# Placing the expert loop of a two-block transformer at an instruction-block boundary on TensorE

## The reference, cut to what matters

```python
logits = (t @ w_router) + b_router                 # 256 tokens, 8 experts
top_v, top_e = lax.top_k(logits, 2)
gate = softmax(top_v)
# for each expert e, over the tokens that chose it:
y += gate * ((silu(x @ w_gate[e]) * (x @ w_up[e])) @ w_down[e])   # 1024 -> 3584 -> 1024
```

## Time and profile before

| what | value |
|---|---|
| median of 3 runs | 3565.04 us (3564.34 to 3575.8) |
| the profiled execution: its time, its span | 3575.8 us, 3574.0 us |
| TensorE matmuls, busy share of the span | 96% |
| mean granted TensorE clock, as a share of 2.4 GHz | 0.964 |
| DMA of weights and data | 637.61 MB |
| packets of the instruction queue q8, bytes | 81, 1.33 MB |

### The profile page before, as it was taken

The page is one execution under the profiler, slowest core; times in us unless marked ns, Lnnn a source line. Parts: engine busy times, 40 slices in busy tenths (PEclk is TensorE's granted clock), DMA queues, the critical chain, the costliest instruction groups (busy, mean ns, idle before and its releaser), DMA issues.

```text
span 3574.0 us, 76004 instructions
## 1 busy us (share of the span) xinstructions
PE 3419.3 (96%) x32714; PEld 2833.5 (79%) x32715; DVE 775.5 (22%) x1802; ACT 679.7 (19%) x1469; POOL 93.0 (3%) x141
## 2 busy tenths in 40 slices
PE   8999799999999999999999999979999999999998
PEld 4456658884557788887788887779999999988898
DVE  1214636650103321213210113230100110011000
ACT  2224122220113321212210111211111111110011
POOL 0000000010001010100000010000000000000000
PEclk9999689999899999999999999979999999999999
DMA  6446012212223243332344442229999998944476
GB/s 271 177 153 236 3 48 83 89 73 73 77 94 113 97 151 132 127 134 103 122 144 141 139 145 106 103 97 370 373 352 371 354 371 346 361 172 153 145 272 264
DMA packets 94763, 637.61 MB, mean 178 GB/s; under 512 B 10784, under 2 KB 11824, under 8 KB 38592
## 3 DMA queue, kind: packets, MB, share of 16 engines
q1 hardware_dynamic: 92048, 627.58, 47.6%
q0 software_dynamic: 2608, 8.49, 0.7%
HBM read 634.98 MB, written 1.05 MB: 178 GB/s over the span
## 4 chain that ended last, share of the span: by engine, by line
PE 93%; DVE 3%; DMA 2%; ACT 2%; issue 1%; SPq 0%; ACTq 0%; DVEq 0%
PE bank L528 24%; PE bank L950 20%; PE bank L620 18%; PE bank L571 7%; PE bank L640 5%; PE bank L542 4%; PE bank L907 2%; PE bank L476 2%; PE bank L502 1%; PE bank L676 1%; PE bank L965 1%; PE bank L658 1%; PE bank L665 1%; DMA ring<-in_moe_down 1%; PE bank L1016 1%
## 5 line engine op out<-in xcount | busy, mean ns | idle before, releaser
L528 PE MATMUL bank<-H,ring 128*128 128x256 f32 (+1 forms) x3040 | 775.0, 417 | 6.9 <-ACT H L1124 6.2
L528 PEld LDWEIGHTS bank<-H,ring 128*128 128x128 f32 x3040 | 580.5, 192 | 185.3 <-issue 112.3
L620 PE MATMUL bank<-PROJ,ring 128*64 128x96 f32 (+2 forms) x7776 | 667.1, 282 | 12.4 <-ACT SC L1173 9.6
L620 PEld LDWEIGHTS bank<-PROJ,ring 128*64 128x64 f32 (+1 forms) x7776 | 547.1, 147 | 131.0 <-issue 96.8
L950 PE MATMUL bank<-MIX,ring 128*64 128x96 f32 x12544 | 524.8, 247 | 8.4 <-issue 7.7
L950 PEld LDWEIGHTS bank<-MIX,ring 128*64 128x64 f32 x12544 | 521.2, 137 | 12.5 <-issue 12.1
L1877 DVE TENSOR_TENSOR PROJ<-SC,bank 128x96 f32 (+2 forms) x246 | 70.9, 288 | 624.2 <-ACT SC L1314 620.0
L950 PE MATMUL bank<-H,ring 128*128 128x256 f32 x896 | 193.7, 379 | 0.0
L950 PEld LDWEIGHTS bank<-H,ring 128*128 128x128 f32 x896 | 170.2, 190 | 23.4 <-issue 0.3
L640 PE MATMUL bank<-H,ring 128*128 128x256 f32 x768 | 178.7, 391 | 3.9 <-ACT PROJ L1195 3.7
L640 PEld LDWEIGHTS bank<-H,ring 128*128 128x128 f32 x768 | 148.5, 196 | 28.4 <-issue 7.7
(11 more groups left out here) (314 smaller groups left out, 2723.4 us busy)
## 6 DMA issues: line engine op xcount, KB each, us to landing
ring<-in_moe_up SPq DMA_DIRECT2D x224, 1024.0 KB, 6.4
ring<-in_moe_down SPq DMA_DIRECT2D x128, 896.0 KB, 6.1
ring<-in_up SPq DMA_DIRECT2D x44, 1024.0 KB, 4.9
ring<-in_mod_b SPq DMA_DIRECT2D x40, 1024.0 KB, 5.9
ring<-in_tproj SPq DMA_DIRECT2D x32, 1024.0 KB, 4.9
ring<-in_proj SPq DMA_DIRECT2D x26, 1024.0 KB, 4.8
ring<-in_gates SPq DMA_DIRECT2D x24, 1024.0 KB, 4.8
ring<-in_down SPq DMA_DIRECT2D x32, 704.0 KB, 4.0
```

Of the source, the lines that this page charges most:

```text
L528: mm = pe.matmul(B[(tile + t) % 4][:, 0:width], w[:, k, t * P:(t + 1) * P], src[:, k, 0:width], start=k == 0, stop=k == k_n - 1)
L620: mm = pe.matmul(B[bank][lo:lo + m, 0:width], w[:, k, lo:lo + m], src(s * half + k), start=s == 0 and k == 0, stop=s == 1 and k == half - 1)
```

## The change

One directive is added for TensorE's stream, between the gather of expert 0 and the loop over the experts:

```diff
                 pe.wait_ge(S("mo_sel"), 1)
                 gather()
+                pe.addr_align(256)
                 with pe.Fori(0, N_EXPERTS) as e:
```

## The result

| | before | after |
|---|---|---|
| median at the first comparison (4 runs each) | 3564.86 us | 3586.14 us |
| ratio | | 1.0051, 95% interval 1.0031 to 1.0072 |
| second comparison (e5 below: 12 and 5 runs) | 3569.38 us | 3587.06 us |
| ratio | | 1.0051, 95% interval 1.0037 to 1.0065 |
| span of the profiled execution | 3574.0 us | 3585.5 us |

The change makes the kernel slower by 0.5%: 0.0051 x 3569.4 = 18.2 us. The forecast was 12.7 us. The direction and the price of the NOPs held; the sum was too small, because a wait that the forecast had counted as 0 came on top. The four runs of before in the first comparison came out low; 27 later runs of it gave 3568.93 us (3563.73 to 3572.86). So 21.3 us between the first two medians is too much, and the second comparison's 17.7 us the better figure.

A forecast was written before the change was run, and what follows sets the result against it. TensorE's stream was taken as the bound: 0 for alignment, +15.8 us for NOPs, -3.1 for cover, 0 for the clock gave +12.7, 3565.0 to 3577.7 us; own range 3575.7 to 3587 us, 8 in 10 about 3564 to 3585.

The forecast's parts named there:

- The bound: Whole kernel: matmuls busy 96% of the span, so delays to TensorE's stream delay the end almost one for one.
- 226 NOPs: Between gather and loop: padding counted from slot 30 of a 256-instruction block to the next slot 0.
- 70 ns for a NOP: TensorE's sequencer ahead of the loop: assumed price of each NOP, giving 15.8 us for all 226.
- 61 ns of handover: Loop head: time between sequencer instructions, from 551 ns unrecorded over nine of them; taken as part of each NOP's price.
- The cheap NOP: Rival on the padding: NOPs under 61 ns can't be told from nothing; all within 0.3%, chance 0.35.
- 3.1 us of cover: Ahead of the loop: NOPs run beside the wait for gathered tokens, hiding 3.1 us and leaving 12.7 us exposed.
- The clock: TensorE's half clock around expert 0's start: 5.6 us after the restart left as is, cost 0, allowance 1.4 us either way.
- The alignment at 0: Loop's place: counted as 0 because the loop stays resident; at most 0.16 us of first branch and 7.7 us idle savable.
- NOPs not executed: Rival on the padding: loader branches over it or it is much shorter; 3565 us, within 0.3%, chance 0.09.
- The aligned head that is faster: Rival at the entry into `up`: aligned place saves at most 10.2 us, reaching 3555 us; chance 0.05.
- the range for 8 in 10: Whole kernel's median: from 3564 us, less a little for scatter, with hidden NOPs, to 3585 us at 102 ns per NOP.
- NOPs of 112 ns: Padding ahead of the loop: upper price of a NOP, +22.2 us, 3587 us; counted with the forecast's own mechanism.

The follow-up runs named there:

- e5: The changed kernel itself, unaltered, timed again beside more runs of the kernel before and profiled: 3587.06 us, ratio 1.0051.
- e1: Changed kernel with the directive asking for slot 30, where the loop already lies, so no NOPs: 3569.96 us, ratio 1.0003 against the kernel before.
- e3: Changed kernel with the loop at slot 128 instead of 0, 98 NOPs: 3577.66 us, ratio 1.0022 against the kernel before.
- e4: Changed kernel with the loop at slot 29, 255 NOPs, 29 in the loop's own block: 3586.07 us, ratio 1.0046 against the kernel before.
- e2: Changed kernel with the loop still at slot 0 but the padding branched over (max_nops=0): 3568.01 us, ratio 0.9996 against the kernel before.
- e8: Same 226 NOPs and slot 0 as the change, but NOPs placed ahead of the router's wait: 3578.18 us, ratio 1.0028 against the kernel before.
- e7: Changed kernel with the loop at slot 16, 242 NOPs, 16 in the loop's block: 3584.56 us, one execution.
- e10: Same 226 NOPs and slot 0 as the change, but NOPs in three parts among the last branch projection's matmuls: 3577.74 us, ratio 1.0021.
- e9: The changed kernel itself, unaltered, profiled once more for its first branch: 3589.6 us, one run.
- e6: Changed kernel with the loop at slot 8, 234 NOPs, 8 in the loop's block: 3586.4 us, one execution.

## Why the forecast was right in kind and too small

**The bound.** TensorE's stream decides, and the local loss passes on to the end. In the profiled executions the 16.9 us at the loop's start show as 11.5 us of span: after, the gather starts 2.1 us earlier (2393.63 against 2395.70 us) and what follows the first matmul of expert 0 is 3.3 us shorter (1166.2 against 1169.5 us). The profiled execution of before was the longest of all its runs (3575.8 us, where 27 later ones lie between 3563.7 and 3572.9). The medians show it in full: 17.7 us.

**226 NOPs.** Exact: 226 in the trace, none in e1 at slot 30, 98 in e3, 255 in e4.

**70 ns for a NOP.** Measured 73 ns: 13 ns recorded and 60 between one and the next. The 61 ns of handover that were worked out from nine other instructions were the term that carried it. The cheap NOP is refuted; it would need under 61 ns, and all runs show 73 to 74. The gap might still hold work that only a traced execution does, as the forecast said; no run here separates that.

**3.1 us of cover.** Right. With 16.5 us of NOPs the local loss without the branch is 16.9 - 3.45 = 13.4 us, 0.7 us over the forecast's 12.7, nearly all of it from the price of a NOP. The idle time between L965 and the first L950 was forecast at 15.5 us and is 14.29 + 5.11 = 19.40 us; the branch is what the forecast did not have.

**The clock.** Right: 5.5 us at half clock after the restart, 5.6 before. e2 and e8 had full clock from before the first `up` phase on, and its matmuls then took 74.5 and 74.3 us; with one profile of each, whether this comes with the kernel or with the execution isn't shown.

**The alignment at 0: this is the term that was wrong.** The forecast said, "I count the alignment itself as 0", and argued from the branches after their first execution and from the missing packets of later experts. For experts 1 to 7 that was right, as e2 shows. But the first execution of the branch at L981, 369 ns, had been read as something that a better place could save, 0.16 us. But its target lies in the next block: between the branch and the gathered `up` stands the dense one, and a round of it is 896 / 7 = 128 matmuls and as many loads, 256 instructions, a whole block. The trace of before could have said when that block comes. Its packet starts at 2396.9 us (the DMA queues of before from 2396.8 to 2397 us):

```profile
q8 instruction: 1, 0.02, 32.8%
```

That is 6.5 us ahead of the branch. The loop's block was entered with the gather, 30 instructions ahead of the MOVE, and the earlier trace rows show idle times of up to 2.37 us when 256 instructions pass in 1.9 us. With the NOPs the loop's block is entered only with the MOVE, 1.5 us ahead of the branch. e4, e7, e8, e10 and e2 enter it 2.7 to 5.0 us ahead and pay at most 0.13 us. Sized from the four profiled executions the term is 1.2 to 3.5 us, 2.3 on average. The sum is 13.4 + 2.3 = 15.7 us; the local times of the four executions (25.67, 23.57, 23.85, 25.22 us) less 8.80 give the same 15.8 us.

**What is left.** The medians say 17.7 to 18.2 us, 2 us more than the local sum, well inside the interval. But e3 (7.9 against 4.1), e8 (10.0 against 6.7), e4 (16.4 against 15.8) and e10 (7.5 against 6.1: 5.7 us in the projection, 0.4 at the loop) err to the same side. For e3 the trace shows most of it, the stop in the first `down`. For the others no profiled execution shows a place: from the first matmul of expert 1 to the end they take 1040.1 to 1044.6 us, against 1045.3 us in the one profiled execution of before and 1043.2 us in e1. A further loss of 1 to 3 us in kernels with added NOPs is possible; it is not shown, and it stays open.

**The rivals.** Cheap NOPs and NOPs not executed are out by the trace. The aligned head that is faster by up to 10.2 us is out by e2 (0.9996, at most 4.6 us faster). The median of 3586.14 us lies 1 us above the range for 8 in 10 (to 3585 us), whose base, three runs of before, was some 4 us low. That it lies within the forecast's own range, to 3587 us, is luck: that end stood for NOPs of 112 ns, and what fills the gap is a low base and a wait for code.

By the rule of the Trainium skill ("Runtime: NRT & Kernel Launch", section "Instruction fetch mechanics") a taken branch whose target is outside the current two-page window waits for a fetch. The first branch does wait for one, with 3.82 us in its row, but its target lies in the next block, inside such a window, and in e5, e9 and e6 the packet had started before the branch. Nor is the two-page window what the later experts show, with branches of 207 to 208 ns over seven blocks. The issue floor of some 20 cycles in the same section is not the price of a NOP of TensorE's sequencer: 73 ns against the prediction's estimate of 16.7.

## What to carry to other kernels

An alignment directive in a stream is not free: its NOPs run, and each takes a handover that the recorded duration doesn't show. Where a loop already stays resident (no instruction packets in later rounds, branches of one length) there was nothing to win, and where the place must be fixed, letting the padding be branched over cost nothing that could be measured here. And a forward jump shortly after a block boundary can wait for the next block: look for that block's packet on the instruction queue and compare its end with the end of the jump. Padding also moves all later boundaries, and one of them can land where its fetch is late, as in e3.

## What the runs showed of the hardware that was not expected

- The same kernel's first branch took 1.60, 1.92, 3.36 and 3.82 us in four executions, because the instruction packet started 0.7 to 2.4 us after the block was entered. The branch ended 1.45 to 1.53 us after the packet's end.
- NOPs of TensorE's sequencer are 73 to 74 ns apart with 13 ns recorded, and 75 of them leave the array idle for 1.6 to 1.8 us amid matmuls whose banks are waited for (e10).
- Branching over 226 slots took 619 ns, once, and ended 1.5 us after the end of the packet on q8 before it (e2).
- With the loop at slot 128, TensorE stopped once for 1.79 us in straight-line matmuls of the first `down`, and the granted clock was half for 3.4 us after it (e3).
